# Moving a projection's part behind the small steps of its round on TensorE, in a hybrid attention and DeltaNet block

## The reference, cut to what matters

```python
h = rmsnorm(x, pre_norm_gain) * (1.0 + scale[:, None, :]) + shift[:, None, :]
proj = h @ w_in          # aq ak av az | iq ik iw | bq bk bv bz beta a | ga gb
q_idx, k_idx = rope(iq), rope(layernorm(ik))            # indexer: 8 heads of 64
score = sum_h w_idx[h] * relu(q_idx[h] @ k_idx.T)       # causal; the 128 best keys stay
o_a = softmax(rope(aq) @ rope(ak).T, over the chosen keys) @ av       # 8 heads of 128
y_a = (o_a * silu(az)) @ w_a_out
q, k, v = silu(causal_conv(bq)), silu(causal_conv(bk)), silu(causal_conv(bv))
o_b = gated_delta_rule_chunked(l2norm(q), l2norm(k), v, g, beta)
y_b = (rmsnorm(o_b) * silu(bz)) @ w_b_out
out = x + gate * rmsnorm((sigmoid(ga) * y_a + sigmoid(gb) * y_b) @ w_o)
```

## Time and profile before

| | us |
|---|---|
| median of 3 runs | 891.04 |
| lowest, highest | 890.91, 892.64 |
| the profiled execution | 892.64 |
| its span, first to last instruction | 890.9 |
| PE busy in the span | 834.9 |
| DVE busy | 472.6 |
| ACT busy | 325.7 |
| POOL busy | 391.5 |
| mean granted TensorE clock | 0.99 |

### The profile page before, as it was taken

One profiled execution on the slowest core, in us unless ns is written; L12 is line 12 of the kernel. 1 busy time (PEld: TensorE's weight loads), 2 busy tenths in 40 slices (PEclk: granted clock), 3 DMA queues, 4 the chain that ended last, 5 costly groups with the idle time before them and its releaser, 6 DMA issues.

```text
span 890.9 us, 11347 instructions
## 1 busy us (share of the span) xinstructions
PE 834.9 (94%) x4240; PEld 672.6 (75%) x4240; DVE 472.6 (53%) x907; ACT 325.7 (37%) x678; POOL 391.5 (44%) x262
## 2 busy tenths in 40 slices
PE   1999778999999899999999999999999999999996
PEld 0557665788888678888888777777877788878996
DVE  2456889745867976666666444335434433232104
ACT  2325433444353444524534433433344322212212
POOL 1124663455364443544634554344543544533442
PEclk9999899999999999999999999999999999999998
DMA  7934530534233341323222322232222254552602
GB/s 284 322 95 143 168 88 1 121 107 114 78 85 80 87 94 51 105 64 92 84 71 56 82 55 69 71 95 71 72 71 71 74 159 145 161 161 81 199 15 95
DMA packets 147345, 92.10 MB, mean 103 GB/s; under 512 B 17746, under 2 KB 140883, under 8 KB 146011
## 3 DMA queue, kind: packets, MB, share of 16 engines
q1 hardware_dynamic: 147290, 91.38, 35.4%
HBM read 84.52 MB, written 6.85 MB: 103 GB/s over the span
## 4 chain that ended last, share of the span: by engine, by line
PE 74%; DVE 17%; ACT 4%; DMA 2%; issue 2%; POOL 1%; SPq 1%; POOLq 0%; ACTq 0%; DVEq 0%
PE ps L588 16%; PE ps L590 16%; PE ps L589 16%; PE ps L629 3%; PE ps L862 2%; DVE yq L1555 2%; DVE kraw L1555 2%; PE ps L910 2%; PE ps L909 2%; PE ps L908 2%; PE ps L849 2%; ACT prob L1147 2%; DMA w_ada_sb<-in_w_ada 2%; DVE binv L1614 1%; PE ps L689 1%
## 5 line engine op out<-in xcount | busy, mean ns | idle before, releaser
L1219 POOL TENSOR_TENSOR w_lo<-raw,w_hi 128x1024 fp32r<-128x1024 f32 (+1 forms) x109 | 263.2, 2420 | 348.4 <-ACT w_hi L929 348.2
L588 PE MATMUL ps<-h_hi,w_hi 128*128 128x512 f32 (+1 forms) x680 | 289.5, 426 | 0.0
L590 PE MATMUL ps<-h_hi,w_lo 128*128 128x512 f32 (+1 forms) x680 | 267.9, 394 | 0.0
L589 PE MATMUL ps<-h_lo,w_hi 128*128 128x512 f32 (+1 forms) x680 | 266.6, 392 | 0.0
L590 PEld LDWEIGHTS ps<-h_hi,w_lo 128*128 128x128 f32 (+1 forms) x680 | 128.2, 188 | 29.3
L588 PEld LDWEIGHTS ps<-h_hi,w_hi 128*128 128x128 f32 (+1 forms) x680 | 128.8, 189 | 25.8 <-issue 3.2
L589 PEld LDWEIGHTS ps<-h_lo,w_hi 128*128 128x128 f32 (+1 forms) x680 | 128.9, 190 | 25.7 <-issue 3.4
L929 ACT ACTIVATE w_hi<-raw 128x1024 fp32r<-128x1024 f32 (+1 forms) x109 | 113.4, 1050 | 17.8 <-PE ps L910 17.1
L1088 ACT ACTIVATE o_tok<-ps 128x128 f32<-128x128 f32 x32 | 8.9, 278 | 124.8 <-PE ps L814 124.6
L629 PE MATMUL ps<-w_ada_sb,cb 128*128 128x512 f32 x64 | 30.7, 642 | 11.7 <-DMA w_ada_sb<-in_w_ada 11.7
L909 PE MATMUL ps<-w_lo,y_hi 128*128 128x256 f32 x128 | 36.2, 283 | 0.0
(11 more groups left out here) (276 smaller groups left out, 1452.4 us busy)
## 6 DMA issues: line engine op xcount, KB each, us to landing
raw<-in_w_in SPq DMA_DIRECT2D x84, 512.0 KB, 3.8
w_ada_sb<-in_w_ada SPq DMA_DIRECT2D x8, 1024.0 KB, 19.7
raw<-in_w_b_out SPq DMA_DIRECT2D x8, 512.0 KB, 4.0
raw<-in_w_a_out SPq DMA_DIRECT2D x8, 512.0 KB, 4.2
ada<-in_w_ada SPq DMA_DIRECT2D x8, 512.0 KB, 4.9
raw<-in_w_o SPq DMA_DIRECT2D x8, 512.0 KB, 4.1
inverse_tiles<-zero SPq DMA_DIRECT2D x2, 1032.0 KB, 5.0
x_sb<-in_x SPq DMA_DIRECT2D x1, 2048.0 KB, 10.2
```

Source lines behind the costliest of these rows:

```text
L588: pe.matmul(out_ap, w_hi[:, slot, k, 0:m], rhs_hi(k), start=(k == 0), stop=False)
L589: pe.matmul(out_ap, w_hi[:, slot, k, 0:m], rhs_lo(k), start=False, stop=False)
L590: mm = pe.matmul(out_ap, w_lo[:, slot, k, 0:m], rhs_hi(k), start=False, stop=(k == KT - 1))
L1219: pool.tensor_tensor(w_lo[:, slot, :, 0:n], raw[:, slot, :, 0:n], w_hi[:, slot, :, 0:n].bitcast(F32), ALU.subtract).then_inc(lo_made, 1)
```

## The change

On PE, the call of `part(r)` moves from the head of the round to its end, behind the small steps and `gate_sum`. All other engines' programs are the same.

```diff
         for r in range(N_ROUNDS):
-            part(r)
             for h in range(HEADS):
                 scan(h, r - R_DELTA[h])
             for h in range(HEADS):
...
             logits(r)
             if r == R_MIX[1] + 6 * KT + 2:
                 gate_sum()
+            part(r)
```

## The result

| | before, us | after, us |
|---|---|---|
| median of 4 runs each | 891.52 | 897.3 |
| lowest, highest | 890.91, 892.64 | 896.52, 897.86 |
| the profiled execution | 892.64 | 897.55 |
| its span | 890.9 | 895.8 |
| mean granted TensorE clock | 0.99 | 0.988 |

The ratio is 1.0062, 95% interval 1.0045 to 1.0081: the kernel became 5.8 us slower. In one number that is inside the range given (892.0 to 899.0) and 2.7 us above its middle case, 894.6.

The account below looks back on a forecast made before the run. It took DVE's order of work to set the pace up to 154.8 us and PE itself from there. Part 1 (1.4) plus part 2 (0.6) on 892.64 gave 894.6 us; range 892.0 to 899.0, 8 in 10.

Parts of the forecast that it names:

- middle case: Whole kernel: 892.64 us plus parts 1 and 2, 2.0 us, giving 894.6.
- the forecast's own case: Whole kernel: parts 1 and 2, with the clock as in the profile or one half-clock stretch less; chance 0.5.
- rival (a): At L665, the longer wait halves PE's clock and delays key 2 further: 899.0, 897.3 or 896.2 us; chance 0.32.
- the judgement on the clock behind L665: At L665, with a wait of 2.4 us: near even whether s6, P6 and P7 run at 1.2 GHz.
- Part 1: From L665 to the last L689 wait: waits not shortened, one part of PE work left behind, +1.4 us.
- Part 2: Key 2's unit: copy and DVE taps 0.5 us late, L1598 and gram 1 0.57 or 0.60 later; +0.6 us.
- the lost turn: DVE's L1499 meets POOL's first L1264 and may lose one turn of about 1.25 us.
- Both together, 2.0: Whole kernel: part 1's 1.4 and part 2's 0.6 us added.
- Its two totals, 899.0 and 897.3: Rival (a): 892.6 + 1.4 + 5.0 = 899.0 us, or 897.3 if the later half-clock stretch is absent.
- Units whose users come later, at nothing: Later units (key 4, key 5, index rows, scan, attention): users not delayed; key 4 costs 0 to 0.3 us.
- The base: Starting time of the sum: the profiled execution's 892.64 us, not the 891.04 median of three runs.
- The guess that quicker runs of before lack a stretch: Kernel before: quicker runs lack the half-clock stretch from 156.0 to 159.2, 1.6 us of work lost at least.

Follow-up runs that it names:

- e2: Against the kernel before: part(r) behind the small steps only in rounds 0 to 6, ahead of them from round 7 on; 895.98 us, ratio 1.0042.
- e8: The changed kernel with POOL's eight L1264 additions cut from 512 to 4 columns, mask of the keys' decay left out; 887.69 us, ratio 0.9962 to the kernel before.
- e5: The kernel before with unread matmuls ahead of PE's long waits (gram 1, gram 3, three L689); 890.19 us, ratio 0.9986.
- e10: Against the kernel before: parts run ahead without fillers, one from the start, four from round 15, six from round 19, given back later; 1092.63 us, ratio 1.2265.
- e11: As e10, with unread matmuls ahead of the first, fifth and eleventh L689; 1096.73 us, ratio 1.2305 to the kernel before.
- e1: Against the kernel before: part(r) ahead of the small steps up to round 6, behind them from round 7 on; 893.25 us, ratio 1.0019.
- e4: Against the kernel before, the opposite change: every small step has one part more ahead of it; 891.22 us, ratio 0.9992.
- e7: The kernel before with POOL's eight L1264 additions cut from 512 to 4 columns, mask of the keys' decay left out; 887.07 us, ratio 0.9953.
- e3: The changed kernel with eight unread matmuls ahead of L665's wait; 894.88 us, ratio 1.0033 to the kernel before.
- e6: The changed kernel with unread matmuls ahead of L665, gram 1, gram 3 and three L689; 892.03 us, ratio 1.0013 to the kernel before.
- e12: Against the kernel before: one part ahead, three from round 15, two from 264, one from 280, plus unread matmuls at long waits; 888.97 us, ratio 0.9972.

## Why the prediction was right or wrong

**The range held, the forecast's own case did not occur.** What occurred is rival (a), which stood at 0.32 against 0.5. The step that failed is the judgement on the clock behind L665: idle times that had made it fall (2.08, 2.41) and one that had not (3.43) were laid side by side, called near even, and then the case of full clock was taken for the forecast. The runs add many waits. Behind 2.29 at L665 it fell in all three profiles that had that wait (after, e2, e8), and 1.94 was enough in e5; behind 2.64 (after, L689 at 144.82) it did not fall. Leaving e10 and e11 aside, whose waits I didn't go through, no profile shows it fall behind idle time of 1.5 or less. In the profile before, three of four waits of 2 us and more had been followed or accompanied by half clock, so the odds should have stood above even for (a). Over before, after, e1 to e4, e7 and e8, PE waited 2 us or longer 30 times behind the prologue, and in 26 of them the clock fell in the wait or right behind it. One and the same wait of L689, 2.62 to 2.64 us long, was followed by half clock in e1, e2 and e4 and not in after, e3 and e8. That the total landed in the range is in part luck: it came by a path that the forecast didn't take.

**Part 1, +1.4:** e1 measured 1.5, and behind the last step of attention after is 1.36 longer than before, e1 1.31. L660, counted from the taps, moved to 71.6 on the old scale and L665 to 82.64 with 2.29 idle, as foretold.

**Part 2, +0.6:** the mechanism was right with full clock (e3, e6): key 2 late by 0.53, a turn lost at L1499 and given back at L1590 and L1594. The size at L1598 is 0.27 and 0.35, half of the 0.57 to 0.60 that I worked out. The term that was too large is the lost turn: put at 1.25, the length of POOL's addition, it cost 0.99 (L1499 took 1.67 in e3 and 0.68 before), while L1590 and L1594 gave 1.27 back.

**Both together, 2.0:** e6 less e5, 1.8 to 2.4.

**Rival (a)'s terms.** Key 2's taps 2.2 late: 2.07. L1495 due at 93.9: 93.78 on the old scale. L1598's end 5.1 late: 3.64. The sum laid whole POOL operations end to end with DVE's, 3 x 1.25 + 2.35 = 6.1 us of turns over the five operations (L1495 to L1560). Measured, the five took 4.7 us over 0.69 each: the first L1264 was 0.5 us under way (91.90) when L1495 started (92.41), and the later turns cost 1.08, 0.98 and 2.04. That accounts for 1.4 of the 1.5. L1590 and L1594 took no turn, as the sum had it. The 5.0 in the sum stands against 4.10 at the last wait. That the half clock does much of its harm by way of the turns was in it, and e8 bears it out for the stretch up to L1598: without the additions the same half clock leaves 0.73 at L1598. Its two totals, 899.0 and 897.3, bracket the median for partly wrong reasons, since the second took a stretch away that after has (158 to 161). That the second equals the measured 897.3 is chance.

**"Units whose users come later, at nothing"** held for key 4 (its copy at 110.40, its taps with no gap), for L798 and for L849. It missed L742, 0.36 us after and in e6, 0.84 in e3, nothing in e1, e2 and e8. It also missed that PE's own work behind the second wait of L701 would run at half clock (120.5 to 123.5); the chain of after passes through the projections there:

```profile
119.01 1.13 PE ps L701 x8
120.14 0.36 PE ps L588
120.50 0.43 PE ps L589
120.92 0.43 PE ps L590
```

So PE was not waiting all the way to the last wait: the parts ahead of gram 4 are on the chain for 5.7 us. Before, the same wait of 3.43 was followed by full clock.

**The base.** The sum was made on 892.64, the slowest of the runs; the median of before was 891.52 then and 891.1 to 891.7 in the four jobs. The guess that quicker runs of before lack a stretch has some support, though not for the stretch named: of 72 runs of the kernel before, 35 with a mean clock of 0.990 or more have a median of 890.88, and 37 with 0.989 or less one of 891.86. Which stretch they lack no run shows.

## What to carry to other kernels

Where PE waits and the time behind the wait is on the path, price the wait twice: its length, and what the work behind it costs at half clock; here a wait that grew by 1.1 us cost 2.4 (by the profiles 3.3) through the clock alone, and eight matmuls that nobody reads took it back. Where two engines take turns on a port, a lateness does not pass through one to one: half a microsecond was half swallowed, two grew to 3.6, so lay the operations of both out in order of time for each lateness in question. Before work is pulled forward into a wait, count for every buffer that it needs in which round the maker's own queue makes it, all the way through the program and not at the wait alone; three parts ahead, with fillers that gain 0.9 alone, gained 2.7 us, six without cost 200.

## What the runs showed of the hardware that I had not expected

- Work that no one reads can make a kernel faster: 8 matmuls ahead of a wait of 2.3 us took 2.4 us off (e3 against after), and 60 of them in e6 took off 5.3 in all (897.3 to 892.0), of which 0.9 to 1.3 would have come off the kernel before too.
- The granted clock fell behind idle times of 1.94 (e5), 2.29 (after, e2, e8) and more, but stayed at 1.00 behind 2.64 (after, before 144.82) and 3.43 (before, 116.74). Behind the same wait of L689, 2.62 to 2.64 us, it fell in three kernels and not in three others. The length of one wait alone does not tell it.
- An operation on DVE of four columns (L1590) takes 0.17 us alone and up to 1.59 beside POOL's w_lo (e12; 1.56 in before, 1.55 after). When key 2 was half a microsecond late, it was such tiny ones that gave a lost turn back.
